# Weight slots with a stride of 4 KB plus 32 bytes, and other SBUF offsets for the split halves of x and hid

## The reference

```python
D_MODEL = 1024; SEQ = 256; DEPTH = 2; D_FF = 2816

def swiglu_ffn(x, w_in, w_out):
    gate, up = jnp.split(x @ w_in, 2, axis=-1)
    return (jax.nn.silu(gate) * up) @ w_out

for l in range(DEPTH):                                   # first block
    h = h + 0.5 * swiglu_ffn(rms_norm(h, ffn1_norm[l]), ffn1_w_in[l], ffn1_w_out[l])
    h = h + hybrid_mixer(...)                            # stick-breaking heads and gated delta rule
    h = h + memory_cross_attention(...)
    h = h + 0.5 * swiglu_ffn(rms_norm(h, ffn2_norm[l]), ffn2_w_in[l], ffn2_w_out[l])
for l in range(DEPTH):                                   # second block
    x = x + 0.5 * swiglu(...)                            # same FFN
    x = x + merged_of_three_attentions(...) @ w_out[l]
    x = x + 0.5 * swiglu(...)
```

## Time and profile before

| | |
|---|---|
| median of 3 runs | 2845.44 us (2845.43 to 2847.02) |
| the profiled execution: its own time | 2846.26 us |
| its span, first to last instruction | 2844.1 us |
| around the span | 2.2 us |
| TensorE busy | 2706.2 us (95%), 14978 matmuls |
| weight loads busy | 2314.8 us (81%) |
| DVE, ACT, POOL busy | 1546.7, 1383.9, 235.2 us |
| mean granted TensorE clock | 0.978 |

### The profile page before, as it was taken

The page is one execution under the profiler, slowest core; times in us unless marked ns, Lnnn a source line. Parts: engine busy times, 40 slices in busy tenths (PEclk is TensorE's granted clock), DMA queues, the critical chain, the costliest instruction groups (busy, mean ns, idle before and its releaser), DMA issues.

```text
span 2844.1 us, 39525 instructions
## 1 busy us (share of the span) xinstructions
PE 2706.2 (95%) x14978; PEld 2314.8 (81%) x14978; DVE 1546.7 (54%) x2107; ACT 1383.9 (49%) x2169; POOL 235.2 (8%) x147
## 2 busy tenths in 40 slices
PE   5999989899999998989999999999999999999998
PEld 3788988778888797877887888888888888878887
DVE  2555654555555567354555555556555555556554
ACT  3445524554454462445444444455544444455543
POOL 1000021000000002100100000243000000244000
PEclk8999999999999999999999999999999999999999
DMA  7654312445555541133654555324555555323554
GB/s 192 199 186 140 119 45 89 134 134 185 185 185 185 163 163 45 61 116 121 218 185 156 186 184 169 116 93 129 190 185 182 187 186 171 120 96 120 195 183 139
DMA packets 118746, 429.23 MB, mean 151 GB/s; under 512 B 12860, under 2 KB 14524, under 8 KB 118204
## 3 DMA queue, kind: packets, MB, share of 16 engines
q1 hardware_dynamic: 116464, 420.27, 45.1%
q10 hardware_dynamic: 2124, 6.71, 1.2%
HBM read 422.74 MB, written 4.19 MB: 150 GB/s over the span
## 4 chain that ended last, share of the span: by engine, by line
PE 87%; DVE 6%; ACT 3%; DMA 2%; issue 2%; ACTq 0%; POOL 0%; SPq 0%; DVEq 0%
PE bank L430 71%; PE bank L450 3%; PE bank L1444 2%; DVE lo_slots L418 2%; DMA raw<-w_full 2%; PE bank L622 1%; PE bank L1491 1%; PE bank L1460 1%; ACT hi_slots L404 1%; PE bank L569 1%; ACT xn L537 0%; PE bank L986 0%; PE bank L768 0%; PE bank L779 0%; PE bank L997 0%
## 5 line engine op out<-in xcount | busy, mean ns | idle before, releaser
L418 DVE TENSOR_TENSOR lo_slots<-raw,hi_slots 128x1024 fp32r<-128x1024 f32 x740 | 914.4, 1240 | 819.8 <-ACT hi_slots L404 819.8
L404 ACT ACTIVATE hi_slots<-raw 128x1024 fp32r<-128x1024 f32 x788 | 830.8, 1057 | 715.8 <-PE bank L430 663.4
L430 PE MATMUL bank<-hi_slots,x_hi 128*128 128x512 f32 x1600 | 636.9, 398 | 19.1 <-DVE lo_slots L395 9.5
L430 PE MATMUL bank<-hi_slots,x_lo 128*128 128x512 f32 x1600 | 626.7, 392 | 0.0
L430 PE MATMUL bank<-lo_slots,x_hi 128*128 128x512 f32 x1600 | 625.8, 391 | 0.0
L430 PE MATMUL bank<-x_hi,hi_slots 128*128 128x256 f32 x1280 | 375.8, 294 | 4.7 <-DVE x_lo L601 3.7
L430 PEld LDWEIGHTS bank<-hi_slots,x_hi 128*128 128x128 f32 x1600 | 302.9, 189 | 83.4 <-issue 12.4
L430 PE MATMUL bank<-x_lo,hi_slots 128*128 128x256 f32 x1280 | 366.7, 287 | 0.0
L430 PE MATMUL bank<-x_hi,lo_slots 128*128 128x256 f32 x1280 | 366.2, 286 | 0.0
L430 PEld LDWEIGHTS bank<-hi_slots,x_lo 128*128 128x128 f32 x1600 | 302.3, 189 | 64.7
L430 PEld LDWEIGHTS bank<-lo_slots,x_hi 128*128 128x128 f32 x1600 | 303.1, 189 | 60.0
(11 more groups left out here) (294 smaller groups left out, 2968.6 us busy)
## 6 DMA issues: line engine op xcount, KB each, us to landing
raw<-w_full SPq DMA_DIRECT2D x792, 512.0 KB, 3.3
bias_rows<-bias_mem ACTq DMA_DIRECT2D x1, 3072.0 KB
bias_mem<-bias_rows SPq DMA_DIRECT2D x1, 2304.0 KB, 11.4
const<-consts ACTq DMA_DIRECT2D x1, 1728.0 KB, 9.8
h<-x_t SPq DMA_DIRECT2D x1, 1024.0 KB, 9.6
mem<-mem_t ACTq DMA_DIRECT2D x1, 1024.0 KB, 4.9
out_t<-h SPq DMA_DIRECT2D x4, 256.0 KB, 2.3
final<-finals ACTq DMA_DIRECT2D x1, 512.0 KB, 13.3
```

What stands on the lines that cost most here:

```text
L404: nc.scalar.activation(w_hi[s], raw[s][:, :], ACT.Copy).then_inc(hi_ready[s], 1)
L418: nc.vector.tensor_tensor(w_lo[s], raw[s][:, :], w_hi[s].bitcast(F32), ALU.subtract).then_inc(lo_ready[s], 1)
L430: mm = nc.tensor.matmul(out, lhsT=a, rhs=b, start=start and n == 0, stop=stop and n == len(passes) - 1)
```

## The change

Only the allocation changes. Each slot of `hi_slots` and `lo_slots` gets 8 unused words at its end, so that the slots are 4096 + 32 bytes apart; `lo_slots` begins 4 words (16 bytes) into its tensor; and four unused tensors of 24, 16, 32 and 24 words stand in front of `x_hi`, `x_lo`, `hid_hi` and `hid_lo`. The instructions, their order, their shapes and their semaphores are the same.

```diff
+HI_STEP, LO_SHIFT = 8, 4
+X_PAD, X_LO_PAD, HID_PAD, HID_LO_PAD = 24, 16, 32, 24
...
-        hi_slots = sb("hi_slots", [P, SLOTS, UNIT], F32R)
-        lo_slots = sb("lo_slots", [P, SLOTS, UNIT], F32R)
-        w_hi = [hi_slots[:, s, :] for s in range(SLOTS)]
-        w_lo = [lo_slots[:, s, :] for s in range(SLOTS)]
+        hi_slots = sb("hi_slots", [P, SLOTS, UNIT + HI_STEP], F32R)
+        lo_mem = sb("lo_slots", [P, LO_SHIFT + SLOTS * (UNIT + HI_STEP)], F32R)
+        lo_slots = lo_mem[:, LO_SHIFT:LO_SHIFT + SLOTS * (UNIT + HI_STEP)].rearrange("p (s n) -> p s n", s=SLOTS)
+        w_hi = [hi_slots[:, s, 0:UNIT] for s in range(SLOTS)]
+        w_lo = [lo_slots[:, s, 0:UNIT] for s in range(SLOTS)]
 
         h = sb("h", [P, TT, D_MODEL])
+        x_pad = sb("x_pad", [P, X_PAD])
         x_hi = sb("x_hi", [P, KT, TOK], F32R)
+        x_lo_pad = sb("x_lo_pad", [P, X_LO_PAD])
         x_lo = sb("x_lo", [P, KT, TOK], F32R)
...
+        hid_pad = sb("hid_pad", [P, HID_PAD], F32, ffn_mem)
         hid_hi = sb("hid_hi", [P, FT, TOK], F32R, ffn_mem)
+        hid_lo_pad = sb("hid_lo_pad", [P, HID_LO_PAD], F32, ffn_mem)
         hid_lo = sb("hid_lo", [P, FT, TOK], F32R, ffn_mem)
```

## The result

The changed kernel takes 2875.01 us (median of 4 runs, 2866.18 to 2876.33) against 2845.43 us: 1.0095 times as long, with an interval of 1.0077 to 1.0113. That is 29.6 us or 1% slower, well beyond the noise. The prediction was 14 us less; its range, 2782 to 2878 us, holds the measured time. The profiled execution took 2873.93 us. The clock is a small part of it: the stretches in which the granted clock is 0.50 add up to 134.8 us, against 124.7 before, and at half the speed the 10.1 us more cost some 5.0 us (an estimate). The execution of 2866.18 us had a mean granted clock of 0.980, above the 0.978 of the kernel before, and was still 20.7 us slower than it.

What follows compares the result with a forecast made beforehand. The prediction took TensorE's matmul count times pitch as the bound. From 2846.3 us it subtracted 14.8 us for hid, other terms 0, giving 2831.5; the median being 0.8 us lower, it forecast 2831 us, range 2782 to 2878 us.

Steps and rivals of the forecast that it cites:

- What bounds the kernel: Whole kernel: TensorE, busy 95% of the span, sets the time as number of matmuls times their pitch.
- The distance is the cause: Up and down products: distance from weights to x or hid explains 227.3 against 234.3 ns with equal instructions.
- the 512-wide term: Matmuls over x and hid: all 6912 at 227.3 ns, so x unchanged and hid 14.8 us less.
- The table modulo 128: Distances after the change: pairs visit 0, 32, 64, 96 (two matmuls in three) or 16, 48, 80, 112.
- 256-wide: The 5168 matmuls of 256 columns: 120.0 ns at both known distances, 0 us; ends 68.7 us less and 0 more.
- Restart after the transposes: Between the four transposes and the 48 products of a group: separate pieces of the chain, 0 us.
- ACT and DVE: Other engines: run at the durations they have now unless their reads meet the matmuls'; 49% and 54% busy.
- x loses its even rhythm: Up product: any distance but 0 costs what 96 costs, up to 33.6 us more, 2879 us; chance 0.37.
- The 16-byte shift: The lo pairs fall to 213.3 ns, 37.2 us less, 2799 us with hid's gain; chance 0.16 including all pairs.
- It cancels: 512-wide matmuls: distance modulo 64 counts, x's loss offsets hid's gain, 1.3 us more, 2847 us; chance 0.17 including no cause.
- The chances: Whole kernel: faster 0.46, same 0.17, slower 0.37; the forecast itself the likeliest single case at 0.30.

Runs made afterwards that it cites:

- e3: Kernel before with 24 unused words in front of x_hi and 1000 in front of hid_hi: x at distance 96, hid left at 96; 2876.5 us.
- e4: Kernel before with 8 unused words in front of hi_slots: everything behind raw moves 32 bytes, distances kept; 2848.77 us.
- e12: Kernel before with four pads: x at 0 within a high or low pair and 128 across, hid the reverse; 2848.08 us.
- e13: Kernel before with w_lo shifted 64 bytes against w_hi, x_lo 64 against x_hi, hid_hi at 64 and hid_lo at 0 from w_hi; 2862.11 us.
- e9: Kernel before with middle-stage weights 64 bytes further into each slot than FFN weights, and hid at 0; 2820.72 against 2844.68 us, 0.9920.
- e14: Changed kernel with HI_STEP = 0: slot step taken back, 16-byte shift and four pads kept; 2872.33 us.
- e8: Kernel before with both slot tensors beginning 4 words in and pads bringing x to 240 and hid to 16; 2863.73 us.
- e2: Kernel before with 552 unused words in front of hid_hi, hid_hi at 0 modulo 4096; 2835.33 against 2846.31 us, 0.9965.
- e7: Kernel before with pads of 56, 32 and 56 words in front of x_hi, hid_hi and y_hi: x 224, hid 192; 2860.40 us.
- e6: Kernel before with pads of 8 words in front of x_hi and of hid_hi: x 32, hid 160; 2871.05 us.
- e5: Kernel before with pads of 48, 8 and 48 words in front of x_hi, hid_hi and y_hi: x 192, hid 64; 2845.82 against 2845.94 us, 0.9999.
- e10: Kernel before with pads of 48, 56 and 40 words in front of x_hi, hid_hi and y_hi: x 192, hid 0; 2830.12 against 2844.68 us, 0.9950.

## Why the prediction went wrong, point by point

- **What bounds the kernel** was read rightly: the pitch makes most of the change, 29.8 - 6.1 - 6.7 = 17.0 us of 27.8 us of span. The other terms, 5.0 us of lower clock and 6.3 us of idle time, stood in no part of the sum.
- **The distance is the cause** was right. e3 and e4 show it: x takes hid's pitch at hid's distance, and moving everything together does nothing. The section "Who interferes with whom" of the page "SBUF — State Buffer" in the Trainium skill, by which TensorE's two reads are independent and it never waits on anyone, forecast no effect; e3 costs 30 us with equal instructions, and the measurement decides. That the two reads are what meets isn't shown.
- **The step that failed** is the 512-wide term: "the row nearest to it is the 227.3 ns of x, and I take that for all 6912". The 227.3 ns belonged to one distance. The map shows that of eight multiples of 32 six cost 233 to 234 ns. Measured, as the mean over the trace: x 233.5 and hid 231.4 ns, +29.8 and -6.1 us where the sum had 0 and -14.8.
- **Under it lay two wrong readings.** The table modulo 128 left x at distance 0 in slot 0. Modulo 256 the pair `x_hi` with `w_hi` is at 128, 96, 64 and 32, and in no slot is any half of x at 0 from any half of the weights. And the table paired a stream with the next load alone, which e12 refutes. With two distances in the trace neither the period nor the pair could be told.
- **hid** won 6.1 us of 14.8. Its `hid_lo` with `w_hi` now visits 0, 224, 192 and 160, its `hid_hi` with `w_hi` 160, 128, 96 and 64. One 0 and one 192 are among them; how they mix isn't understood (e13).
- **256-wide**, taken at 0 us with nothing more as the bad end, gained a little: 117.2 ns in the stretch shown, 118.6 in the mean, 6.7 us in all. Two distances with equal means, 0 and 96, had looked like no effect; at 192 the stretch of e9 has 113.5 ns, and e14 shows that they can also get slower, to 121.3.
- **Restart after the transposes** at 0 us was right, 0.44 us as before. **ACT and DVE** keep their durations (1240 and 1058 ns for a split, 1240 and 1057 before), but the sum left out what a shift of time does to them: the 6.3 us of idle time.
- **The rivals.** "x loses its even rhythm" is what happened, by the sign it named: runs of 48 at 11.1 to 11.25 us and uneven steps. Its 2879 us is 4 us above the measured time, and part of that nearness is luck: it left hid and the 256-wide matmuls where they were, which won 12.8 us, and had neither the idle time nor the lower clock, which cost 11.3. The 16-byte shift freed nothing (e8). "It cancels" was wrong: modulo 64 isn't the period, and the gain over hid is a fifth of the loss over x.
- **The chances.** The text gave a reason against taking x's pitch for all, that the rhythm existed at distance 0 only, and the forecast took it all the same because it was the nearest row. Of two known distances the one with the even rhythm was the special one.

## What to carry to other kernels

When two equal instruction streams differ in pitch, move one operand alone by a few multiples of 32 bytes, as e2 and e3 do; one pad can be worth 11 us or cost 30 us here. Do it for each shape apart, since the best distance of 512-wide matmuls (0 modulo 256) isn't that of 256-wide ones (192 among those tried), and keep all slots and both halves at the same residue: those are the cases that the map covers. An even rhythm in a tuned kernel is worth protecting: six of the eight residues tried here are bad, and a layout that visits many of them loses it. Count the time at the lower clock in both kernels before you put a difference down to the pitch.

## What was unexpected of the hardware

- The pitch of a 512-wide fp32r matmul goes by the distance between weights and activations modulo 256 bytes: 227.0 ns at 0, 229.0 to 229.4 at 192, 233.3 to 234.3 at 32, 64, 96, 128, 160 and 224. Moving everything by 32 bytes changes nothing (e4), and at the lower clock 0 and 96 cost the same, 426.3 ns (before and e3).
- 256-wide matmuls follow another map: 120.0 ns at 0 and at 96, and 113.5 ns in a stretch of e9 at 192. As the mean of all steps with x moving it is 119.9 at 0 and 96, 118.4 at 224 (e7), 117.2 at 32 (e6) and 115.0 to 115.2 at 192 (e5, e10). At the lower granted clock, 0.50 or 1.2 GHz, their pitch was 213.6 ns, one column a cycle. The Trainium skill's page "TensorE: Matmul & The Clock Gate", section "Back-to-back issue gap", gives N / 2.4 + 2.5 ns for an isolated warm matmul, 215.8 ns at 512 columns; no run of 48 or 240 here has a mean under 226.8 ns.
- A DVE instruction on one column took 2.32 us instead of 0.15 when it started just behind a POOL split of 2.34 us. A change that shifts the engines by 0.1 us can cost or save 2 us at such a place.
